# Reordering the attention units of a two-layer decoder trunk

## The reference, cut to what matters

```python
p_c = masked_softmax(s, cmp_end[None, :] <= t[:, None])      # compressed: 31 keys
o_c = jnp.einsum('bgrqn,bngd->bqgrd', p_c.astype(qb.dtype), vc)
...
o_s = jnp.einsum('bgrqm,bgqmd->bqgrd', p_s, v_g)             # selected blocks
...
o_w = jnp.einsum('bgrqk,bkgd->bqgrd', p_w, vwb)              # sliding window
return gb[..., 0:1] * o_c + gb[..., 1:2] * o_s + gb[..., 2:3] * o_w
```

## Time and profile before

| | |
|---|---|
| runs | 1568.66, 1572.69, 1575.97 us; median 1572.69 |
| profiled execution, its own time | 1577.8 us |
| its span | 1576.0 us |
| TensorE busy | 1520.8 us, 96% |
| mean granted clock | 0.986 of 2.4 GHz |
| attention on TensorE | from 147.68 (end of `tkc`) to 267.37 (first transpose of `to`) us |

### The profile page before, as it was taken

How to read it: one execution, slowest core, us unless ns; L and a number is a source line. 1 busy time by engine, 2 the same in 40 slices (tenths; PEclk the granted TensorE clock), 3 DMA queues, 4 the chain that set the end, 5 groups by cost and what they waited for, 6 DMA issues and landing times.

```text
span 1576.0 us, 21250 instructions
## 1 busy us (share of the span) xinstructions
PE 1520.8 (96%) x7810; PEld 1280.9 (81%) x7810; DVE 549.6 (35%) x904; ACT 608.3 (39%) x1207; POOL 671.8 (43%) x514
## 2 busy tenths in 40 slices
PE   7999999999999999999999999899899999999998
PEld 7888988888788888888888776688788888888886
DVE  2742575532461111101016379945336110111014
ACT  3344544254424333333233468634432332333221
POOL 4452000563255444444464554452242445444442
PEclk9999899999999999999999999999999999999999
DMA  8532000342034333332332422232122333333222
GB/s 218 131 102 70 1 1 9 106 148 86 31 105 153 101 94 97 89 105 95 101 115 93 147 80 80 94 114 87 54 87 64 100 98 100 93 100 94 100 94 93
DMA packets 113265, 147.05 MB, mean 93 GB/s; under 512 B 20262, under 2 KB 69664, under 8 KB 113184
## 3 DMA queue, kind: packets, MB, share of 16 engines
q1 hardware_dynamic: 112864, 145.87, 30.2%
q0 software_dynamic: 320, 0.08, 0.0%
HBM read 143.80 MB, written 2.10 MB: 93 GB/s over the span
## 4 chain that ended last, share of the span: by engine, by line
PE 87%; DVE 6%; ACT 4%; POOL 1%; issue 1%; DMA 1%; SPq 0%; DVEq 0%; ACTq 0%
PE ps L604 78%; PE ps L805 3%; PE ps L769 2%; PE ps L785 2%; PE ps L609 1%; POOL w_lo L569 1%; ACT fm_hi L1010 1%; ACT px L1248 1%; PE ps L836 1%; PE ps L761 1%; DVE h L1612 1%; PE ps L731 0%; ACT w_hi L986 0%; DMA w_raw<-in_x_wkv 0%; DMA x_res<-in_x 0%
## 5 line engine op out<-in xcount | busy, mean ns | idle before, releaser
L569 POOL TENSOR_TENSOR w_lo<-w_raw,w_hi 128x512 fp32r<-128x512 f32 (+1 forms) x452 | 606.2, 1350 | 875.2 <-ACT w_hi L986 872.2
L986 ACT ACTIVATE w_hi<-w_raw 128x512 fp32r<-128x512 f32 (+1 forms) x452 | 278.9, 627 | 597.1 <-PE ps L604 561.8
L604 PE MATMUL ps<-fm_hi,w_hi 128*128 128x512 f32 (+1 forms) x1096 | 420.0, 383 | 7.2 <-ACT fm_hi L1010 4.8
L604 PE MATMUL ps<-fm_lo,w_hi 128*128 128x512 f32 (+1 forms) x1096 | 418.4, 382 | 0.0
L604 PE MATMUL ps<-fm_hi,w_lo 128*128 128x512 f32 (+1 forms) x1096 | 418.2, 382 | 0.0
L604 PEld LDWEIGHTS ps<-fm_hi,w_hi 128*128 128x128 f32 x1096 | 208.2, 190 | 49.5 <-ACT fm_hi L1010 5.5
L604 PEld LDWEIGHTS ps<-fm_lo,w_hi 128*128 128x128 f32 x1096 | 208.2, 190 | 39.2 <-issue 0.5
L604 PEld LDWEIGHTS ps<-fm_hi,w_lo 128*128 128x128 f32 x1096 | 208.2, 190 | 39.0
L1712 DVE TENSOR_TENSOR gf<-silu,ps 128x512 f32<-128x512 f32 x44 | 28.3, 684 | 433.0 <-ACT silu L1278 410.4
L1484 DVE SCALAR_TENSOR_TENSOR x_res<-x_res,ps 128x512 f32<-128x512 f32 x48 | 31.4, 685 | 276.1 <-PE ps L604 190.8
L604 PE MATMUL ps<-w_hi,g_hi 128*128 128x512 f32 x288 | 112.0, 389 | 0.0
(11 more groups left out here) (279 smaller groups left out, 2215.4 us busy)
## 6 DMA issues: line engine op xcount, KB each, us to landing
w_raw<-in_f_w_up SPq DMA_DIRECT2D x352, 128.0 KB, 2.1
w_raw<-in_f_w_down SPq DMA_DIRECT2D x88, 256.0 KB, 2.6
w_raw<-in_x_wkv SPq DMA_DIRECT2D x64, 256.0 KB, 3.1
w_raw<-in_o_w_in SPq DMA_DIRECT2D x40, 256.0 KB, 2.6
w_raw<-in_x_wq SPq DMA_DIRECT2D x32, 256.0 KB, 2.7
w_raw<-in_x_wo SPq DMA_DIRECT2D x32, 256.0 KB, 2.7
w_raw<-in_e_w_in SPq DMA_DIRECT2D x24, 256.0 KB, 2.9
w_raw<-in_o_w_out SPq DMA_DIRECT2D x20, 256.0 KB, 2.6
```

Source lines behind the costliest of these rows:

```text
L569: nc.gpsimd.tensor_tensor(lo[:, :n], w_raw[:, c % RING, :n], hi[:, :n].bitcast(F32), ALU.subtract).then_inc(w_split, 1)
L604: last = nc.tensor.matmul(outp, lhsT, rhs, start=(clear and k == 0 and n == 0), stop=(k == steps - 1 and n == 2), skip_group_check=True)
L986: nc.scalar.activation(w_pair(c)[0][:, :n], w_raw[:, s, :n], ACT.Copy).then_inc(w_rounded, 1)
```

## The change

```diff
-UNITS = [u for qb in range(TT) for u in
-         [(qb, "cmp", 0, HEADS)] + [(qb, b, hh, UNIT_HEADS[qb]) for b in ("sel", "win")
-                                    for hh in range(0, HEADS, UNIT_HEADS[qb])]]
+def block_units(qb, b):
+    return [(qb, b, hh, UNIT_HEADS[qb]) for hh in range(0, HEADS, UNIT_HEADS[qb])]
+
+def in_turn(wide, narrow):
+    return [u for pair in itertools.zip_longest(wide, narrow) for u in pair if u]
+
+def compressed(qb):
+    return [(qb, "cmp", 0, HEADS)]
+
+UNITS = in_turn(block_units(3, "sel"), block_units(0, "sel") + block_units(0, "win") + compressed(0) + block_units(1, "sel")[:1])
+UNITS += in_turn(block_units(3, "win"), block_units(1, "sel")[1:] + compressed(3) + compressed(1) + block_units(1, "win")[:1])
+UNITS += in_turn(block_units(2, "sel"), block_units(1, "win")[1:])
+UNITS += in_turn(block_units(2, "win"), compressed(2))
+ADDED = [u for u, (_, b, _, _) in enumerate(UNITS) if b != "sel"]
...
-                last = turn(ps[:, b0 + g, 0:NCMP], kc_dup[:, g, :, :].rearrange("p a d -> p (a d)"), NCMP)
+                last = turn(ps[:, b0 + 2, g * NCMP:(g + 1) * NCMP], kc_dup[:, g, :, :].rearrange("p a d -> p (a d)"), NCMP)
...
-            evacuated("tkc")
+            evacuated("cmp")
...
             scores(0)
+            evacuated("tkc")
             scores(1)
...
-            pe.wait_ge(o_ready, len(UNITS) - TT)
+            pe.wait_ge(o_ready, len(ADDED))
...
-            for g in range(KV_HEADS):
-                nc.scalar.activation(kcT[:, g, :], bank("tkc", g)[:, 0:NCMP], ACT.Copy).then_inc(evac_a, 1)
+            nc.scalar.activation(kcT[:, :, :].rearrange("p g n -> p (g n)"), bank("tkc", 2)[:, 0:KV_HEADS * NCMP], ACT.Copy).then_inc(evac_a, 1)
...
-                if b == "cmp":
+                if b == "sel":
                     nc.vector.tensor_tensor(dst.rearrange("p (r d) -> p r d", d=HD), o, wb, ALU.mult).then_inc(o_evac, 1)
```

More of the change, by code:

```diff
@@ L24 @@
 from contextlib import ExitStack
+import itertools
 import numpy as np
@@ L116, in plan_groups @@
     g += [("ein0", KT, 4, 0), ("tm", 0, 4, 4), ("ein1", KT, 4, 0), ("ein2", KT, 4, 0), ("ein3", KT, 4, 0)]
-    g += [("k0_0", KT, 4, 0), ("mix", 0, 4, 4), ("tq0", 0, 2, 2), ("tq1", 0, 2, 2), ("tk", 0, 4, 4), ("cmp", 0, 3, 0), ("k0_1", KT, 4, 0), ("tkc", 0, 2, 0)]
+    g += [("k0_0", KT, 4, 0), ("mix", 0, 4, 4), ("tq0", 0, 2, 2), ("tq1", 0, 2, 2), ("tk", 0, 4, 4), ("cmp", 0, 3, 0), ("k0_1", KT, 4, 0), ("tkc", 0, 1, 0)]
     g += [("attn", 0, 0, 0), ("to", 0, 4, 4)]
@@ L170 @@
 UNIT_HEADS = [8, 4, 2, 2]
-UNITS = [u for qb in range(TT) for u in
-         [(qb, "cmp", 0, HEADS)] + [(qb, b, hh, UNIT_HEADS[qb]) for b in ("sel", "win")
-                                    for hh in range(0, HEADS, UNIT_HEADS[qb])]]
+def block_units(qb, b):
[9 more added lines that the diff above has]
+ADDED = [u for u, (_, b, _, _) in enumerate(UNITS) if b != "sel"]
+FIRST_CMP = [b for _, b, _, _ in UNITS].index("cmp")
 GATE_OF = {"cmp": 0, "sel": 1, "win": 2}
```

## The result

The changed kernel takes 1577.48 us (median of 17 runs, 1573.73 to 1581.45), the kernel before 1570.48 (17 runs, 1565.83 to 1577.24). The ratio is 1.0044, interval 1.0032 to 1.0057: slower, by 7 us, and just within the half per cent set as the bound, which the interval's upper end passes. The forecast was 1573.2, +0.5.

A forecast was written before the change was run, and what follows sets the result against it. TensorE, busy 1520.8 of 1576.0 us, was taken as the bound. Terms summed to -3.9 us without a clock fall; one fall (+4.4) made +0.5, so 1572.69 became 1573.2, range 1566.5 to 1580.

The forecast's parts named there:

- rival B: In attention the clock does not fall at all: -3.9 us, chance 0.22.
- rival C: In attention, waits behind narrow units keep pulling the clock down: one further stretch +5.2 us (chance 0.10), two +10.0 (0.08).
- (a): At attention's entry, TensorE's idle gap waiting for the copy of the compressed keys goes: -1.25 us.
- (d): Before the first weighing, TensorE waits for unit 0's copy, queued behind unit 1's eight-head exponentials on ScalarE: +2.7 us.
- (e): At unit 2's weighing, TensorE waits for ScalarE's copy, queued behind the next unit's exponentials: +1.1 us, bounds 0 and 1.3.
- (c): Addition to `o_tok` moves from selected to compressed units, relieving VectorE in block 2: -0.4 us.
- (f): TensorE waits for VectorE's copy behind units that add: +2.9 us for 512-column outputs, +0.6 for half-width ones.
- (b): Two low-clock stretches in attention, 4.75 us lost in each, disappear if the clock never falls: -9.5 us.
- (h): The idle wait at attention's start most likely brings the clock down once: +4.4 us, making the sum +0.5.
- A: One fall of the clock in attention, about 10 us at clock 0.50: +0.5 us, chance 0.50.
- D: No fall in attention, and waits at unit 2 and for VectorE's copies vanish: -8.5 us, 1564.2, chance 0.10.

The follow-up runs named there:

- copy first: The changed kernel, but ScalarE copies unit 0's turned probabilities before the exponentials of unit 1: ratio 1.0058 to the kernel before, median 1581.55 us.
- GpSimd additions: The changed kernel with additions to the output made by GpSimd, VectorE making only the product into two alternating temporaries: ratio 1.0051 to the kernel before, median 1579.06 us.
- the block order: The changed kernel with its units by query block again (selected, window, compressed), everything else as changed: ratio 1.0029 to the kernel before, median 1575.32 us.

## Why the prediction came out as it did

The range held and so did "the same by half a per cent", but 7.0 measured against +0.5 is a miss in size, and the sign of the real difference was left open. There was luck in both. The range was wide enough for rival B's gain and for the first step of rival C, and the ratio's interval ends at 1.0057, past the bound.

**(a)**, the entry gap: right, gone, and the moved wait costs nothing. **(d)**, 2.7 at the start: 2.61 and 2.59. **(e)**, 1.1: 1.34 and 1.33. **(c), (f)**: 3.1 forecast for the short waits after taking off (c). The profile after lists 0.29, 0.16, 0.16, 0.38, 0.34, 0.21, 0.27 = 1.81 us of them, and 0.60, 0.84 and 0.84 at the last three weighings, where before had 0.74 and 0.73: 2.6 more in all. Every wait that was named is there. Those behind eight-head units are a third to two thirds of their size: behind W0 0.29 and behind C0 and C3 0.16 each, not 0.48; behind C1 0.38, not 0.6; behind C2 0.60, not 0.9. Those behind W1a and W1b are 0.34 and 0.21, where 0.6 was forecast for both. Without the clock the terms sum to -1.25 - 0.4 + 2.7 + 1.1 + 2.9 + 0.6 = +5.65. At full clock the measured difference is +5.8, and at equal clock, over many runs, about 5. That the sum comes so near is in part luck: the waits that the profiles list differ by -1.25 + 2.61 + 1.34 + 2.62 = 5.3, and where the other half microsecond lies was not traced.

**(b)** failed: "-9.5" as what the change could win back from the clock. The pricing per stretch was sound: 119.69 - 110.89 = 8.8 us lost in the first profile's two stretches. But the step took one execution's low clock as the kernel's own. The 102 other runs have a mean clock of 0.9899 where that execution had 0.986, which by the slope of its runs is 6.4 us of time. Not all of that is attention's: windows of 1 us over the whole span show 23 and 20 us at 0.50 outside attention in the two profiles of before, and 21 in both of the changed kernel. A mean clock of 0.9899 is some 32 us at 0.50 in all, which leaves 8 to 12 for attention. At 0.43 each, a typical run thus has about 4.4 us there to win back, not 9.5 (an estimate from these figures). The sum was made against that execution's 1577.8 and then shifted to the median by 5.1, which moved the base and left the 9.5 in the difference. With 4.4 in its place the same working gives +5.6.

**(h)**, one fall behind the start wait: right for the place in both profiles (154 us; and it goes when the wait is filled). It was priced at 4.4 and cost 119.92 - 116.70 = 3.2 in the first profile, with 6.8 us at 0.50 where A expected about 10. As a count it was too few: the second profile has three stretches, 13.7 us, which cost 5.3. The mean clock of the changed kernel's 24 runs is 0.9889, 0.001 below before, or 1.7 us. With the 4.9 at equal clock that makes up the 6.6 us between the means of all runs.

**The rivals.** Of the two profiles, one has more falls than A's: two further stretches of 3.4 us each, together less than the one of about 10 us that C's first step priced. C had waits pulling the clock down. The stretch at 212 came without any; what brought the one at 174 is not shown; those at 167 and 166 us in two of the experiments stand close behind a wait. As the cause of a lower mean clock, though, waits do not hold. Taking them away (copy first, GpSimd additions) was each time followed by a lower mean clock, 0.9853 and 0.9864, and dense products raised it, clearly in the old order (by 0.0020, and again in the repeat), less surely in the new (by 0.0023). The rule cited from the Trainium skill, "TensorE: Matmul & The Clock Gate", section "HAM oscillation — how this bites in real kernels", that bursts parted by waits return to half clock, is told there of DMA waits of some 3 to 5 us, longer than any wait here, so naming each wait of (d) to (f) a candidate went further than the page. The stretch at 154 us, behind 2.61 us of idle time, is like it; the one at 212 is not. D was wrong: the copies' lateness did not vanish. B did not occur in either profile.

What stays open is why the copy-first kernel and the block order have so much lower a clock than the changed one. Runs of small products are there in all of them, and moving the stage by a microsecond or two may change where a fall begins; nothing here separates the two.

## What to carry to other kernels

Before a stretch of low clock in a profile is booked as something to win, look at several executions: here one profile had 20.5 us of it in this stage, the next of the same kernel 13.6. That the profiled run was 5.1 us above the median was the warning, and the mean clock listed with each run shows why. Price the order of a software pipeline at one fixed clock, from who waits for whom, and the clock apart; the first came within 0.2 us here, in part by luck, and the second was off by 5. When wide and narrow units alternate, check the narrow unit's longest step on a side engine (eight exponentials, 2.8 us, plus what leads up to them) against what the main engine has left to do until it needs the neighbour's copy queued behind that step (3.8 us).

## What the runs showed of the hardware

The granted clock fell to 0.50, at 212 us above, with TensorE busy throughout; what it had run just before were only products of 31 to 128 columns. Dense needless products put beside such runs of small ones raised the mean clock (0.9918 to 0.9938 in the old order, and in the new 0.9894 to 0.9917, on fewer runs), and won back about the time that they cost and no more. In attention a microsecond at the low clock cost 0.43 us (8.8 for 20.5; 0.39 to 0.47 over four profiles). And one unchanged kernel had executions from 1565 to 1579 us, which followed its mean clock by 1.63 us for each 0.001.
